# Last three expert units added through PSUM, the other units' rows loaded meanwhile

## The reference

```python
h = rms_norm(x)                                   # 512 tokens x 1024
grp_p, grp_idx = top_k(softmax(h @ w_rg + b_rg), 1)       # best of 4 groups
top_logits, top_local = top_k(in_group_logits, 2)         # best 2 of its 4 experts
weights = grp_p * softmax(top_logits)                     # two weights per token
out[t] = sum over its 2 experts e of weight * (silu(h@w_gate[e]) * (h@w_up[e])) @ w_down[e]
y = rms_norm(x + out, norm_final_w)
```

## Time and profile before

| | us |
|---|---|
| median of 3 runs | 700.14 |
| the profiled execution, its own time | 698.2 |
| its span, first to last instruction | 696.5 |
| PE busy (share of the span) | 644.4 (93%) |
| PE weight loads busy | 535.8 (77%) |
| DVE busy | 473.3 (68%) |
| ACT busy | 394.0 (57%) |
| POOL busy | 176.3 (25%) |
| mean granted TensorE clock | 0.968 of full |

### The profile page before, as it was taken

The page is one execution under the profiler, slowest core; times in us unless marked ns, Lnnn a source line. Parts: engine busy times, 40 slices in busy tenths (PEclk is TensorE's granted clock), DMA queues, the critical chain, the costliest instruction groups (busy, mean ns, idle before and its releaser), DMA issues.

```text
span 696.5 us, 9239 instructions
## 1 busy us (share of the span) xinstructions
PE 644.4 (93%) x3371; PEld 535.8 (77%) x3372; DVE 473.3 (68%) x779; ACT 394.0 (57%) x664; POOL 176.3 (25%) x217
## 2 busy tenths in 40 slices
PE   5999999999999999999999998899999999999910
PEld 4688788788878888888888885788878888887810
DVE  4778995265521434425665549899999999998717
ACT  6449583355624233243432443388898898987623
POOL 7000009981000000000000002145545546455210
PEclk9999999999999999999999997699999999999975
DMA  8524343213222222113235615468787797866335
GB/s 270 178 67 96 61 106 121 62 60 76 66 61 62 61 61 60 62 61 95 88 121 223 260 62 191 164 196 287 216 272 249 224 313 240 292 225 216 104 140 241
DMA packets 73729, 104.63 MB, mean 150 GB/s; under 512 B 31634, under 2 KB 53203, under 8 KB 73555
## 3 DMA queue, kind: packets, MB, share of 16 engines
q1 hardware_dynamic: 60912, 95.57, 42.3%
q0 software_dynamic: 12672, 8.43, 4.0%
q10 hardware_dynamic: 98, 0.03, 0.0%
HBM read 123.90 MB, written 17.83 MB: 203 GB/s over the span
## 4 chain that ended last, share of the span: by engine, by line
PE 83%; DVE 7%; DMA 3%; ACT 2%; POOL 2%; issue 2%; SPq 0%; POOLq 0%; ACTq 0%; DVEq 0%
PE bank L1582 22%; PE bank L1584 22%; PE bank L1583 22%; PE bank L1983 2%; PE bank L1718 2%; PE bank L1907 1%; PE bank L1628 1%; DVE down_lo L1351 1%; DMA expert_rows<-expert_rows_hbm 1%; PE bank L1787 1%; PE bank L1777 1%; PE bank L1737 1%; DMA ew_raw<-in_w_down,extra_weight_rows 1%; PE bank L1750 1%; DVE rank_onehot L1466 1%
## 5 line engine op out<-in xcount | busy, mean ns | idle before, releaser
L1582 PE MATMUL bank<-h_hi,w_hi 128*128 128x512 f32 x304 | 123.1, 405 | 1.0 <-POOL index_row_i L662 1.0
L1584 PE MATMUL bank<-h_hi,w_lo 128*128 128x512 f32 x304 | 118.7, 390 | 0.0
L1583 PE MATMUL bank<-h_lo,w_hi 128*128 128x512 f32 x304 | 118.5, 390 | 0.0
L1351 DVE TENSOR_TENSOR gate_up_lo<-ew_raw,gate_up_hi 128x1024 fp32r<-128x1024 f32 x92 | 108.3, 1219 | 10.6 <-ACT gate_up_hi L950 8.4
L950 ACT ACTIVATE gate_up_hi<-ew_raw 128x1024 fp32r<-128x1024 f32 x92 | 92.2, 1056 | 9.1 <-DMA ew_raw<-in_w_gate,extra_weight_rows 7.8
L1037 DVE TENSOR_TENSOR w_lo<-w_raw,w_hi 128x2048 fp32r<-128x2048 f32 x26 | 60.2, 2317 | 50.1 <-ACT w_hi L744 50.0
L1582 PE MATMUL bank<-gate_up_hi,unit_in_hi 128*128 128x512 f32 x184 | 76.7, 417 | 0.0
L1584 PE MATMUL bank<-gate_up_hi,unit_in_lo 128*128 128x512 f32 x184 | 72.9, 396 | 0.0
L1583 PE MATMUL bank<-gate_up_lo,unit_in_hi 128*128 128x512 f32 x184 | 72.6, 394 | 0.0
L718 POOL TENSOR_TENSOR ffn_in_T<-ffn_in_T,norm_ffn_b 128x1024 f32<-128x1024 f32 x1 | 2.3, 2346 | 261.5 <-ACT ffn_in_T L968 261.5
L1582 PEld LDWEIGHTS bank<-h_hi,w_hi 128*128 128x128 f32 x304 | 57.2, 188 | 12.3 <-issue 1.5
(11 more groups left out here) (361 smaller groups left out, 1335.8 us busy)
## 6 DMA issues: line engine op xcount, KB each, us to landing
w_raw<-in_w_in SPq DMA_DIRECT2D x17, 1024.0 KB, 5.2
ew_raw<-in_w_gate SPq DMA_DIRECT2D x32, 512.0 KB
ew_raw<-in_w_up SPq DMA_DIRECT2D x32, 512.0 KB
ew_raw<-in_w_down SPq DMA_DIRECT2D x32, 512.0 KB
w_raw<-in_w_out SPq DMA_DIRECT2D x4, 1024.0 KB, 5.0
expert_rows<-expert_rows_hbm SPq DMA_DIRECT2D x8, 512.0 KB, 7.3
x_T<-in_x SPq DMA_DIRECT2D x4, 512.0 KB, 4.9
w_raw<-in_w_in SPq DMA_DIRECT2D x8, 256.0 KB, 4.2
```

The lines of the kernel that those rows point to most:

```text
L1351: dve.tensor_tensor(dst, eraw[slot][:, :], hi.bitcast(F32), ALU.subtract).then_inc(elo_done, 1)
L1582: pe.matmul(out_ap, lhs_hi, rhs_hi, start=first, stop=False)
L1583: pe.matmul(out_ap, lhs_hi, rhs_lo, start=False, stop=False)
L1584: return pe.matmul(out_ap, lhs_lo, rhs_hi, start=False, stop=last)
```

## The change

1. The units 20, 21 and 22 (`LATE`) are not scattered to HBM any more. ACT and DVE copy their result from PSUM, scaled by the weight of each row (`l_w`), as a high and a low part. PE multiplies both with a 0/1 matrix (`l_oh`, row of the unit to token of the tile), and sums the three units in PSUM for each of the four tiles (`late_rows`): 4 tiles x 3 units x 2 halves x 2 parts = 48 matmuls of 128x512. DVE adds the two banks of each tile to `y` (`add_late`). Unit 22's down product goes to banks 2 and 3 instead of 5 and 6.
2. SP waits only for the scatters up to unit 19 before it loads the pairs; they have other places in SBUF. DVE does the first multiply-adds inside iterations 22 and 23, the others between the late steps.
3. What this needs: 16 DMAs of 256 KB write zeros to `o_rows` during the input projections; 8 DMAs write the weights to `wt_rows` in HBM at SP's u = 4; POOL gathers the 3 x 128 weights after `spread(12)`; DVE builds the 0/1 matrices in iteration 6 (`late_onehots`).

```diff
 # SP, input projections
+                if 4 <= u < 8:
+                    for r_ in range(2 * (u - 4), 2 * (u - 4) + 2):
+                        for half in range(2):
+                            sp.dma_start(o_rows[P * r_:P * (r_ + 1), S * half:S * (half + 1)],
+                                         sub_t[:, :, :].rearrange("p i c -> p (i c)")).then_inc(zero_rows, 16)
 # SP, expert loop
             for u in range(1, UNITS - 1):
+                if u == 4:
+                    sp.wait_ge(ids_done, EARLY)
+                    for k, w in enumerate((w1, w2)):
+                        for t in range(TT):
+                            r0 = S * k + P * t
+                            sp.dma_start(wt_rows[r0:r0 + P, :], w[:, t:t + 1]).then_inc(wt_out, 16)
...
-            sp.wait_ge(ot_out[(UNITS - 2) % 2], 16 * ((UNITS - 2) // 2 + 1))
-            sp.wait_ge(ot_out[(UNITS - 1) % 2], 16 * ((UNITS - 1) // 2 + 1))
-            sp.wait_ge(gu_ps, UNITS)
+            for i in range(2):
+                u = LATE[0] - 1 - i
+                sp.wait_ge(ot_out[u % 2], 16 * (u // 2 + 1))
             for t in range(TT):
+                if t == 2:
+                    sp.wait_ge(gu_ps, UNITS - 1)
...
 # POOL
-                spread(u)
+                if u < LATE[0]:
+                    spread(u)
+                if u == 12:
+                    pool.wait_ge(wt_out, 16 * 2 * TT)
+                    pool.wait_ge(ids_done, EARLY + 4)
+                    for i, v in enumerate(LATE):
+                        nc.gpsimd.indirect_dma_start(
+                            out=l_w[:, i:i + 1], out_offset=None, in_=wt_rows[:, :],
+                            in_offset=bass.IndirectOffsetOnAxis(ap=ridx[:, SEQ[v], 0:1], axis=0),
+                            bounds_check=2 * S - 1, oob_is_err=False).then_inc(wt_in, 16)
                 load_extra(KIND_G, u + 4)
 # ACT
+            def late_out_hi(i):
...
+                for h in range(2):
+                    act.activation(l_hi[i][:, S * h:S * (h + 1)], ps[down_banks(u)[h]][:, :], ACT.Copy,
+                                   scale=l_w[:, i:i + 1]).then_inc(late_hi, 1)
...
-                if u >= 2:
+                if 2 <= u < UNITS - 1:
                     unit_out(u - 2)
+                if u == UNITS - 1:
+                    late_out_hi(0)
...
-            unit_out(UNITS - 1)
+            late_out_hi(1)
+            late_out_hi(2)
 # DVE
+            def late_onehots():
+                dve.tensor_copy(row_f[:, :], row_i[:, :])
+                for i, u in enumerate(LATE):
+                    ins = dve.tensor_copy(l_row[:, i:i + 1], ridx[:, SEQ[u], 1:2])
+                link(ins)
+                for t in range(TT):
+                    ins = dve.tensor_scalar(l_col[:, :, t], l_row[:, :], -float(P * t + 255), None, ALU.add)
+                link(ins)
+                for i in range(3):
+                    ins = dve.tensor_tensor(l_oh[i][:, :, :], bc_mid(row_f[:, :], TT), bc_last(l_col[:, i, :], P), ALU.is_equal)
+                ins.then_inc(late_set, 1)
+            def late_out_lo(i):
...
+                for h in range(2):
+                    hs = slice(S * h, S * (h + 1))
+                    dve.wait_ge(late_hi, 2 * i + h + 1)
+                    dve.scalar_tensor_tensor(l_lo[i][:, hs], ps[down_banks(LATE[i])[h]][:, :], l_w[:, i:i + 1],
+                                             l_hi[i][:, hs].bitcast(F32), ALU.mult, ALU.subtract).then_inc(late_lo, 1)
+            def add_pair(t, k):
+                dve.wait_ge(pair_in[t], 32)
+                link(dve.scalar_tensor_tensor(y[:, t, :], pair[t][k][:, :], (w1, w2)[k][:, t:t + 1], y[:, t, :], ALU.mult, ALU.add))
...
+                if u == UNITS - 1:
+                    add_pair(0, 0)
+                    late_out_lo(0)
+                if u == UNITS:
+                    add_pair(0, 1)
...
                     extra_units()
+                if u == 6:
+                    late_onehots()
...
+            late_out_lo(1)
+            add_pair(1, 0)
+            add_pair(1, 1)
+            late_out_lo(2)
+            add_pair(2, 0)
+            add_late(0)
+            add_pair(2, 1)
+            add_late(1)
+            final_norm(0)
+            add_pair(3, 0)
+            add_late(2)
+            final_norm(1)
+            add_pair(3, 1)
+            add_late(3)
+            final_norm(2)
+            final_norm(3)
 # PE
+            def late_rows(t, i):
+                pe.wait_ge(late_lo, 2 * i + 2)
+                for n_ in range(2):
+                    ns = slice(S * n_, S * (n_ + 1))
+                    o = ps[late_bank[t][n_]][:, :]
+                    pe.matmul(o, l_oh[i][:, t, :], l_hi[i][:, ns], start=i == 0, stop=False)
+                    ins = pe.matmul(o, l_oh[i][:, t, :], l_lo[i][:, ns], start=False, stop=i == 2)
...
             hidden_f(UNITS - 1)
+            pe.wait_ge(late_set, 1)
+            late_rows(0, 0)
             down(UNITS - 1)
+            late_rows(0, 1)
+            late_rows(1, 0)
+            late_rows(0, 2)
+            late_rows(1, 1)
+            late_rows(1, 2)
+            for t in range(2, TT):
+                for i in range(3):
+                    late_rows(t, i)
```

More of the change, by code:

```diff
@@ L196, in build @@
         nffn = at("norm_ffn_b", [P, D], F32, r_tmp + 8192)
-        pair = [at(f"expert_rows{k}", [P, TT, D], F32, r_main + 16384 * k) for k in range(2)]
-        out_t = at("out_T", [P, TT, D], F32, ffn_raw)
+        out_t = at("out_T", [P, TT, D], F32, r_main)
+        junk_f = at("square_junk_final", [P, D], F32, r_main + 16384)
+        late_hi_at = (r_h + 8192, r_h + 12288, r_h + 24576)
+        late_lo_at = (r_h + 4096, r_h, r_h + 28672)
+        l_hi = [at(f"late_out_hi{i}", [P, D], F32R, o) for i, o in enumerate(late_hi_at)]
+        l_lo = [at(f"late_out_lo{i}", [P, D], F32R, o) for i, o in enumerate(late_lo_at)]
+        row_f = at("index_row_f", [P, P], F32, r_b + 11264)
         hot = [at(f"rank_onehot{i}", [P, P, 16], BF16, r_o + 4096 * i) for i in range(2)]
@@ L285, in build @@
         brg = new("router_bias", [P, NG + NE])
+        l_oh = [at(f"late_onehot{i}", [P, TT, P], F32R, r_tmp + 2048 * i) for i in range(2)]
+        l_oh.append(new("late_onehot2", [P, TT, P], F32R))
+        l_row, l_col, l_w = new("late_rows", [P, 3]), new("late_rows_by_tile", [P, 3, TT]), new("late_weights", [P, 3])
         row_rep = at("index_row_repeated", [P, P, 16], BF16, tri_at)
@@ L496, in build, with down_banks @@
         o_rows = nc.dram_tensor("expert_rows_hbm", (2 * S, D), F32)
+        wt_rows = nc.dram_tensor("slot_weights_hbm", (2 * S, 1), F32)
+        free_slot = place(KIND_D, LATE[0], 0)
+        pair_at = [[r_tmp + 8192, r_o], [r_o + 4096, None]] + [[gu_at[UNITS % 2] + 8192 + 16384 * h + 4096 * k for k in range(2)] for h in range(2)]
+        pair = [[eraw[free_slot[0]] if o is None else at(f"expert_rows{t}_{k}", [P, D], F32, o) for k, o in enumerate(ks)]
+                for t, ks in enumerate(pair_at)]
+        late_bank = ((7, 1), (0, 4), (5, 6), (2, 3))
+        def down_banks(u):
+            return (2, 3) if u == UNITS - 1 else (5, 6)
         w_gate_v = a["w_gate"][0].rearrange("e (p k) f -> e p (k f)", p=P)
@@ L1556, in _, with add_late @@
                         one_hots(EARLY + u)
-            def add_experts(t):
-                dve.wait_ge(pair_in[t], 32)
-                link(dve.scalar_tensor_tensor(y[:, t, :], pair[0][:, t, :], w1[:, t:t + 1], y[:, t, :], ALU.mult, ALU.add))
-                dve.scalar_tensor_tensor(y[:, t, :], pair[1][:, t, :], w2[:, t:t + 1], y[:, t, :],
-                                         ALU.mult, ALU.add).then_inc(tok_added, 1)
+            def add_late(t):
+                dve.wait_ge(late_ps, t + 1)
+                for n_ in range(2):
+                    ns = slice(S * n_, S * (n_ + 1))
+                    ins = dve.tensor_tensor(y[:, t, ns], y[:, t, ns], ps[late_bank[t][n_]][:, :], ALU.add)
+                ins.then_inc(tok_added, 1)
             def final_norm(t):
@@ L1570, in final_norm @@
                                          ALU.mult, ALU.mult).then_inc(fin_done, 1)
-            add_experts(0)
-            for t in range(1, TT):
-                add_experts(t)
-                final_norm(t - 1)
-            final_norm(TT - 1)
+            late_out_lo(1)
[14 more added lines that the diff above has]
+            final_norm(3)
         @block.tensor
@@ L2004, in down @@
                 pe.wait_ge(hid_lo, u + 1)
-                if u:
+                if u == UNITS - 1:
+                    pe.wait_ge(xs_lo_done, UNITS)
+                elif u > LATE[0]:
+                    pe.wait_ge(late_lo, 2 * (u - LATE[0]))
+                elif u:
                     pe.wait_ge(ot_done, u)
@@ L2010, in down @@
                     for f in range(2):
-                        ins = three(ps[5 + n_][:, :], ea_hi[:, f, :], ea_lo[:, f, :], w_hi[:, f, ns], w_lo[:, f, ns],
```

(1 more changed line is left out.)

22 lines of the change are left out of this document (19 added, 3 removed).

## The result

The changed kernel took 710.50 us (median of 4 runs, 707.51 to 711.09) against 699.32 for the kernel before on the same chip (4 runs): 1.0152 times as long, interval 1.0125 to 1.0179. A time given for a run is the median of all its executions, and is set against the kernel before on the same chip (698.63 to 699.63); the ratios leave out slow executions, over 1.5% above the fastest of their kernel, which are three of mended2's twelve. The prediction was 698.7 with a range of 694.5 to 703.5. The profiled execution took 711.09, its span is 709.4.

What follows compares the result with a forecast made beforehand. The prediction took PE's queue to bound the middle and a chain without slack the end. End -8.2, matrices +2.9 and gathers +3.9 gave -1.4 from the median 700.14: 698.7 us, range 694.5 to 703.5.

Steps and rivals of the forecast that it cites:

- The eight weight writes: SP's iteration 4: they fall into SP's idle time, take up to 5.8 us, and add nothing to the sum.
- What costs nothing: Part of the forecast listing zero writes, weight writes, POOL's wait for the zero writes and fewer scatters, all at no cost.
- the sum with all bounds: End, iteration 6 and gathers added at their extreme values: from -4.5 to +5.1 us against the median.
- The three gathers, +3.9: POOL after `spread(12)`: three gathers of 1.3 us delay unit 16's gate load, reaching PE whole, +3.9 us.
- the bound of 6.8: Upper bound in us for the gathers' cost, if each takes 1.95.
- My lower bound: Gathers' cost of 2.0 us, if unit 16's gate load transfers faster when it comes later and alone.
- `late_onehots`, +2.9: DVE's iteration 6: building the matrices ahead of unit 5's `hidden_lo` becomes PE idle time, +2.9 us, bounds 1.9 and 3.5.
- The clock falls in the new stalls: Rival, 15%: PE's clock halves in iterations 6 and 15, costing 2.4 us per stall, for 703.5 in all.
- My reason against it: Against the clock falling: the idle times in iterations 6 and 15 are below the 5.1 us seen to be harmless.
- The end, -8.2: After the last `hidden_lo`: scatters and loads leave the path, DVE runs without a gap, 8.2 us gained, range 5.2 to 8.4.
- The zero writes, 0: Zero writes of 4 MB go out with the projections' loads 4 to 7, where ACT waits for PE: no cost.
- 11% for slower: Chance of a time above 703.6: half of the falling-clock rival and a quarter of the longer-queue rival.

Runs made afterwards that it cites:

- mended2: The changed kernel with weights transposed and written by two DMAs in iteration 7, gathers spread singly, matrices in iteration 22, tile 0's adds later: 697.97 us.
- no_writes: The changed kernel without the eight weight writes; the gathers read elements of the input x instead: 703.49 us.
- before_writes: The kernel before plus only the eight weight writes at SP's iteration 4, read by nothing: 709.74 us.
- before_wide: The kernel before plus eight writes at SP's iteration 4, each 4 rows of 512 bytes, read by nothing: 700.07 us.
- warm: The changed kernel with filler matmuls on PE before the down products that stall, 8 in iteration 6 and 24 in iteration 15: 709.37 us.
- no_gathers: The changed kernel with the weight writes but without the three gathers, late rows scaled by 1: 702.42 us.
- mended3: The changed kernel with transposed weights copied by ScalarE, two four-row writes, gathers spread, matrices in iteration 22, tile 0's adds later: 693.26 us.
- end_only: The changed kernel without weight writes and gathers, late rows scaled by 1, matrices built in iteration 22: 693.70 us.

## Why the prediction was wrong, step by step

- **The eight weight writes, put under "What costs nothing" with "the next load goes out at most 1.2 later": the step that failed.** I priced them by SP's issue time. SP's time was as forecast (4.3 us, nothing late), but behind the 1024 four-byte elements the loads' packets stood in the DMA queues. Taken out, they are worth 7.0 us (no_writes), alone 11 (before_writes), and with wide elements nothing (before_wide). With 7 in place of 0 the sum would have been 705.7, outside the range. No row of the trace before had such a write, and for an operation that the trace doesn't show I should have kept an upper bound on its transfer; the 1.2 bounded the issue alone, and not even that was in the sum with all bounds.
- **The three gathers, +3.9.** The queue time was right (4.1), of which 3.1 reached the load's last issue. The term was mis-sized by what comes after: the load took 3.2 us longer to land, with SP's load now among it, and the clock gave 2.3 more (warm). These make 8.6; 7.8 shows in the interval and 8.1 by no_gathers, above the bound of 6.8. My lower bound took the late load to come alone; it came together with SP's.
- **`late_onehots`, +2.9.** VectorE: 2.66. PE's gap was 2.32, not 3.4 (3.24 in no_writes). The interval grew 3.5 all the same, since the clock added 1.5.
- **"The clock falls in the new stalls", 15%.** The rival came true in both of its places, beside the forecast's own terms, at 1.5 and 2.3 us (I had priced 2.4), and in the stall of iteration 4 too. My reason against it was wrong: at the end of the kernel before the clock fell 5.1 us after the last matmul, and I took shorter idle times to be harmless. In the loop it fell 3.3 us after the last dense matmul, when PE was already working again for 1 us. Nor does the length of the idle time alone settle it: ahead of the down product of unit 19 PE stood 2.25 us in before_wide and 2.43 in no_writes with the clock staying at full, and 2.20 in mended3, where it fell.
- **The end, -8.2.** 21.5 us from the last `hidden_lo`, exactly as summed: 8.5 less than before. But that point was to come 0.3 us late and came 1.5 late, counted from `hidden_T(21)` (12.95 us against 11.47), because tile 0 was there 1.3 us later than the sum had it. So the end gave 7.0 in this execution, within the 3 us allowed for. end_only shows 5.7 by its median.
- **The zero writes, 0.** Right: no shift at the first unit (+0.3), and ACT's wait is still PE's.

Set against the forecast of -1.4, the change came out at +11.2 (710.50 - 699.32), a miss of 12.6. By the medians the writes are 7.0 of it, the gathers 4.2 (8.1 for 3.9), the end 2.5 (5.7 for 8.2), and the matrices take 1.2 back (1.7 for 2.9, where the 1.7 is what the other runs leave). The writes alone put the time outside the range: without them it is 703.49.

With all its bounds the sum reached 705.2, and the range I gave stopped at 703.5. The chances went with the sum: 11% for slower came from cases of the terms that I had, and the missing term was in none of them.

## What to carry to other kernels

Price a transfer by its elements as well as by its bytes and its issue: a column of a [128, n] tile written to DRAM is 128 elements of 4 bytes, and here the loads behind it paid in SP's queue and in POOL's. Transposed on PE into four rows of 512 bytes the same data cost nothing that shows (mended3 at 693.26 with them, end_only at 693.70 without). A queue that gets late can also let another queue's load go first: look at what is issued in the time between. And where a new PE wait appears in a dense stretch, add the matmuls behind it at half clock as a case of its own, also where it is only 2 to 3 us long.
